# A two-block transformer forward pass: the work region of on-chip memory starts at a multiple of 2,048 bytes

## What is computed

```python
def first_block(x, ...):                     # two layers
    for i in range(2):
        h = x @ w_in[i]                      # q, k, v of three kinds of attention, and gates
        merged = sum(gate_b * (o_b @ w_up_b[i]) for b in (fox, sb, dsa))
        x = layer_norm(ALPHA * x + merged @ w_out[i], ...)
        ffn = jnp.square(jax.nn.relu(x @ w_ff_in[i])) @ w_ff_out[i]
        ple = jax.nn.sigmoid(x @ w_ple_gate[i]) * (p[i] @ w_ple[i])
        x = layer_norm(ALPHA * x + ffn + ple, ...)
    return x

def second_block(x, c, ctx, ...):            # two layers, x and the context xc side by side
    for layer in range(2):
        x  = x  + 0.5 * mx[2] * swiglu(modulate(rms_norm(x, ...), mx[0], mx[1]), w_in, w_out)
        xc = xc + ...                        # the same with the context's modulation
        ox, oc = mla_mixer(...) if layer == 0 else swa_mixer(...)
        x = x + mx[5] * ox                   # and xc
        x = x + 0.5 * mx[8] * swiglu(...)    # and xc, but not in the last layer
    return rms_norm(x, final_norm_g)
```

## The kernel before

| tensor | offset in work, KiB | bytes of one row |
|---|---|---|
| x_hi, x_lo | 0, 8 | 1,024 |
| h_hi, h_lo | 0, 16 | 2,048 |
| un_hi | 32 | 2,048 |
| un_lo | 54.5 | 2,048 |
| f_hi, f_lo | 16, 48 | 1,024 |
| o_hi, o_lo | 59, 65 | 1,024 |
| cq_hi, cq_lo; om_hi, om_lo | 44, 52; 48, 64 | 2,048 |

## Time and profile before

### The profile page before, as it was taken

The page is one execution under the profiler, slowest core; times in us unless marked ns, Lnnn a source line. Parts: engine busy times, 40 slices in busy tenths (PEclk is TensorE's granted clock), DMA queues, the critical chain, the costliest instruction groups (busy, mean ns, idle before and its releaser), DMA issues.

```text
span 3014.3 us, 45553 instructions
## 1 busy us (share of the span) xinstructions
PE 2801.8 (93%) x17432; PEld 2378.3 (79%) x17432; DVE 1566.5 (52%) x2334; ACT 1097.7 (36%) x1415; POOL 0.2 (0%) x4
## 2 busy tenths in 40 slices
PE   7899999999998996999988998999989999889897
PEld 6788799987878995887866576878868788677897
DVE  5676565557765656243255445342353433566555
ACT  3253344334435534223232334222232322335543
POOL 0000000000000000000000000000000000000000
PEclk9999899999998998999999899999999999999998
DMA  8666567585675772242332012242332423311463
GB/s 246 191 206 202 166 218 220 153 253 165 205 249 165 224 215 70 60 118 83 88 92 85 15 43 72 74 114 70 105 96 64 114 77 97 98 56 31 140 187 105
DMA packets 585222, 394.25 MB, mean 131 GB/s; under 512 B 43686, under 2 KB 579140, under 8 KB 584900
## 3 DMA queue, kind: packets, MB, share of 16 engines
q1 hardware_dynamic: 585028, 391.62, 44.0%
HBM read 390.54 MB, written 1.05 MB: 130 GB/s over the span
## 4 chain that ended last, share of the span: by engine, by line
PE 86%; DVE 8%; ACT 3%; issue 2%; DMA 1%; DVEq 0%; ACTq 0%; SPq 0%
PE bank L1856 86%; DVE w_lo L1153 2%; ACT w_hi L849 1%; DMA xs<-in_mod_w 1%; DVE t L1168 1%; DVE xs L1168 1%; DVE t L1161 1%; ACT t L853 0%; DVE h_lo L1168 0%; DMA raw<-in_w_in 0%; DVE qk L1161 0%; DVE acc L1161 0%; DVE t L1165 0%; ACT x_hi L853 0%; ACT h_hi L853 0%
## 5 line engine op out<-in xcount | busy, mean ns | idle before, releaser
L1153 DVE TENSOR_TENSOR w_lo<-raw,w_hi 128x2048 fp32r<-128x2048 f32 (+3 forms) x338 | 689.9, 2041 | 352.9 <-ACT w_hi L849 350.8
L849 ACT CAST w_hi<-raw 128x2048 fp32r<-128x2048 f32 (+3 forms) x338 | 575.0, 1701 | 618.9 <-PE bank L1856 602.4
L1856 PE MATMUL bank<-h_hi,w_hi 128*128 128x512 f32 (+1 forms) x1560 | 574.9, 369 | 52.1 <-DVE h_lo L1168 41.0
L1856 PE MATMUL bank<-h_lo,w_hi 128*128 128x512 f32 (+1 forms) x1560 | 572.9, 367 | 0.0
L1856 PE MATMUL bank<-h_hi,w_lo 128*128 128x512 f32 (+1 forms) x1560 | 572.3, 367 | 0.0
L1856 PE MATMUL bank<-x_hi,w_hi 128*128 128x256 f32 x1344 | 384.1, 286 | 26.6 <-DVE x_lo L1168 13.5
L1856 PEld LDWEIGHTS bank<-h_hi,w_hi 128*128 128x128 f32 x1560 | 297.8, 191 | 113.5 <-issue 48.5
L1856 PE MATMUL bank<-x_lo,w_hi 128*128 128x256 f32 x1344 | 375.8, 280 | 0.0
L1856 PE MATMUL bank<-x_hi,w_lo 128*128 128x256 f32 x1344 | 375.6, 279 | 0.0
L1856 PEld LDWEIGHTS bank<-h_hi,w_lo 128*128 128x128 f32 x1560 | 297.5, 191 | 52.6
L1856 PEld LDWEIGHTS bank<-h_lo,w_hi 128*128 128x128 f32 x1560 | 297.7, 191 | 52.1
(11 more groups left out here) (278 smaller groups left out, 3921.4 us busy)
## 6 DMA issues: line engine op xcount, KB each, us to landing
raw<-in_ffn_w_in SPq DMA_DIRECT2D x176, 512.0 KB
xs<-in_mod_w SPq DMA_DIRECT2D x72, 1024.0 KB, 5.5
raw<-in_ffn_w_out SPq DMA_DIRECT2D x64, 704.0 KB
raw<-in_w_in SPq DMA_DIRECT2D x40, 1024.0 KB
raw<-in_w_ff_in SPq DMA_DIRECT2D x32, 1024.0 KB
raw<-in_w_ff_out SPq DMA_DIRECT2D x32, 1024.0 KB
raw<-in_w_out SPq DMA_DIRECT2D x8, 1024.0 KB
raw<-in_w_ple_gate SPq DMA_DIRECT2D x8, 1024.0 KB
```

The source lines that it names most:

```text
L849: act.copy(w_hi[s][:, w], raw[s][:, w]).then_inc(hi_made, c.did(hi_made))
L1153: dve.tensor_tensor(w_lo[s][:, w], raw[s][:, w], w_hi[s][:, w].bitcast(F32), ALU.subtract).then_inc(lo_made, c.did(lo_made))
L1856: ins = pe.transpose(o, l, r) if transpose else pe.matmul(o, l, r, start=start, stop=stop)
```

## The change

Three of the small tables, `cols_mod` (576 bytes), `cond_st` (1,024) and `small` (256), are no longer allocated among the fixed ones but behind the work region. Together they are 1,856 bytes. Everything that was allocated behind them moves down: `cols_d`, `bf`, `ln_cols`, `mods` by 576, `cond` by 1,600, and `amod` to `top8`, `t1` to `t3`, `rings_8` and `work` by 1,856. `work` becomes 131,072, a multiple of 2,048, and so do `t1` (118,784), `t2` and `t3`. The tensors in the work region keep their offsets in it, so x_hi, h_hi, h_lo, un_hi, f_hi, cq and om now start at multiples of 2,048, o_hi and o_lo (odd KiB) 1,024 above one, and un_lo (54.5 KiB) 512 above one. The chunk slots, `xs` and the constants stay where they are. The three tables now start at 227,328, 227,904 and 228,928. No instruction is added, removed or moved, on any engine: the lists of instructions of both programs, with their waits, are the same row by row.

```diff
@@ -510,18 +510,13 @@
         cols_a = fixed("cols_a", [P, 120])
-        cols_mod = fixed("cols_mod", [P, LAYERS, 72])
         cols_d = fixed("cols_d", [P, 22])
...
-        cond_st = fixed("cond_st", [P, KT, P // COL_GROUPS])
         cond = fixed("cond", [P, 2, KT])
-        small = fixed("small", [P, 64])
-        one = small[:, 2:3]
-        stat = [small[:, 8 + 8 * b:16 + 8 * b] for b in range(3)]
         amod = fixed("amod", [P, KT, 2])
...
         work = top[0]
+        assert work % 2048 == 0
+        top[0] += 94 * 1024
+        cols_mod = fixed("cols_mod", [P, LAYERS, 72])
+        cond_st = fixed("cond_st", [P, KT, P // COL_GROUPS])
+        small = fixed("small", [P, 64])
+        one = small[:, 2:3]
+        stat = [small[:, 8 + 8 * b:16 + 8 * b] for b in range(3)]
+        assert top[0] <= nc.sbuf_usable_end
+        cond_cols = cond_st[:, :, 0:2].rearrange("p k c -> p c k")
...
-        assert work + 94 * 1024 <= nc.sbuf_usable_end, (work, nc.sbuf_usable_end)
```

More of the change, by code:

```diff
@@ L618, in build @@
         ident, ones, rot, fold = (const(cst, n) for n in ("ident", "ones", "rot", "fold"))
-        cond_cols = cond_st[:, :, 0:2].rearrange("p k c -> p c k")
         mod_slot = xs[:, :, S:2 * S]
```

## The result

| | median, us | lowest to highest | runs |
|---|---|---|---|
| before | 3023.21 | 3004.14 to 3029.62 | 6 |
| after | 3036.45 | 3032.36 to 3041.06 | 6 |

The ratio is 1.0056, with a 95% interval of 1.0030 to 1.0082, which is 0.56% or some 17 us; the two medians lie 13 us (0.44%) apart, and against the 75 later runs of the kernel before (median 3018.2 us) the changed one is 18 us slower. The kernel became a little slower: about what the prediction called the least that can be told from no change (0.5%, 15 us), and on the side to which it had given 0.15. The profiled execution took 3036.57 us, its span 3034.8 us, with a mean granted clock of 0.964 (before: 3014.3 us and 0.957).

What follows compares the result with a forecast made beforehand. TensorE's distance between matmul starts was taken to bound the kernel. All terms were 0, added to the profiled 3016.1 us; 3020 us was forecast, between that and the 3021.9 median, with a range of 2930 to 3040.

Steps and rivals of the forecast that it cites:

- The bound: Long stages: TensorE, busy 93% of the span, sets the end by how closely matmuls follow one another.
- The tables, VectorE, ScalarE and the DMAs at 0: Moved tables, vector and scalar work on the region, and transfers: each costed at 0.
- The first two observations against a cost of crossing a multiple of 2,048: Matmul starts: un_lo and un_hi both 0.23 us; 256-column rows, crossing or not, equal within some 3 ns per matmul.
- The moving operand of the matmuls: Streamed rows in the work region: new addresses cost 0; bounds 0 and 90 us gained.
- The prediction's own sign of being wrong: Matmul start distances: wrong if that of 512 or 256 columns moves by more than 3 ns.
- the slower rival: 256-column matmuls: streamed rows at multiples of 128 take 4.4 ns more on 6,816, 30 us, 3050 us; chance 0.15.
- The third argument under it: Matmul surplus of 6.7, 11.1 and 20.0 ns: grows with columns streamed, not a toll at one place of the row.
- The faster rival: 512-column matmuls: aligned rows stop crossing and lose their surplus, 60 to 90 us, some 2945 us; chance 0.42.
- The two rules: Skill on TensorE: N/2.4 + 2.5 ns between matmuls, an estimate of 79 us lower; two read ports independent.

Runs made afterwards that it cites:

- before + 64: The kernel before, tables where they were, with only the work region 64 bytes higher (1920 above a multiple of 2048); 3015.13 us, ratio 0.9988.
- slots and region + 64: The changed kernel with chunk slots and work region both 64 bytes higher; 3036.28 us, ratio 1.0061 to the kernel before.
- slots + 64: The changed kernel with chunk slots 64 bytes higher, work region still at the multiple of 2,048, hgate moved behind it; 3004.23 us, ratio 0.9958.
- region + 64: The changed kernel with only the work region 64 bytes higher, the three tables still behind it; 3009.18 us, ratio 0.9965 to the kernel before.

## Why the prediction was wrong

**What held.** The bound: TensorE alone sets the end, and an address can only matter through the distance between starts. The tables, VectorE, ScalarE and the DMAs at 0: their rows didn't change. The first two observations against a cost of crossing a multiple of 2,048 held as well. Un_lo still crosses and costs what un_hi does, and at "before + 64" every wide row crosses and the wide matmuls have their best pace.

**The step that failed** is the term "The moving operand of the matmuls", costed at 0 "by the nearest rows, those where a crossing can be seen to cost nothing". The rows showed that a crossing costs nothing. They didn't show that an address costs nothing, and the step took the one for the other. The term measured 8,000 times 5.0 ns less 5,310 times 0.6 ns, 40 less 3, some +37 us. The prediction's own sign of being wrong, a distance of 256 columns that moves by more than 3 ns, came about: 5.0 ns, and eighteen starts in 2.13 us, where it had 2.04 for itself and 2.12 for the slower rival. That the 3036 us lie under the 3040 at which its range ended is luck: the range took in only half the way to the slower rival's price, and it held because the time from which its sum starts lies some 15 us above what the distances of the kernel before give.

**The third argument under it** ("the surplus grows with the columns streamed") read 6.7, 11.1 and 20.0 ns as one law. At a distance of 0 both widths have the same surplus, 13.3 ns (120.0 less 106.7, 226.7 less 213.3). From distance 192 to 0 the narrow matmuls lose 6.6 ns and the wide ones gain 6.6. There is no one surplus that an alignment takes away. At half the clock neither width has any: the median distances are 427 and 213 ns, before and after, against 426.7 and 213.3 for the columns alone.

**The slower rival** had the right rows and the right price: 117.6 ns where weights are streamed against 113.3 for activations, 4.4 ns on 6,816 matmuls, 30 us. It measured 5.0 ns on 8,000. Its rule was wrong (the moving operand's residue modulo 128: "slots and region + 64" has the quick residue and 118.7 ns, and "slots + 64" has the region at the same place as the changed kernel and is 32 us quicker). Where weights are streamed past activations, the distance has the other sign, 64 instead of 192, and "slots + 64", which gives the activations that distance, has 117.0 ns: rows 9 were a sample of another distance. The sentence that held it down, that rows 8 show the slow kind at the quick residue as well, was a fact and still is: at distances of 64 and of 192 both kinds occur, while at 0, 128 and 224 no group of 24 starts has a mean under 115 ns. What makes a tile the one or the other at 192 wasn't found. But an exception in a minority of tiles says little against a rival about the majority, and 0.15 was too low for a price read directly off two groups of rows.

**The net of 13 us** (18 against all runs) instead of 37 isn't a correction of the term. It comes of the kernel before, which lies some 15 us above what its distances give (table above); in the profiled pair, 17 us net go to stretches at half the clock. Against "region + 64" the loss is 27 us. The forecast of 3050 for this rival would have stood nearer to the measured time than that of 3020 only by a few us: 14 against 16.

**The faster rival**, crossing as the surplus, gave 2945 us and was wrong in its mechanism: rows of h and un_hi no longer cross and gained 0.6 ns. Yet its thought that 512 columns could be had quicker was right: 6.6 ns of 20.0, by the distance from the loaded weights.

**The two rules.** The best pace of wide matmuls in any run was 226.7 ns and of narrow ones 113.4. The Trainium skill ("TensorE: Matmul & The Clock Gate", section "Back-to-back issue gap") has N/2.4 + 2.5, which is 215.8 and 109.2; no layout tried here reaches either. That section calls the formula the gap of an isolated matmul, which the prediction didn't say, and gives a sustained stream of loads and matmuls about 131 ns at 512 columns; no run here shows such a pace. The Trainium skill ("SBUF — State Buffer", section "Who interferes with whom") lists TensorE's two read ports, for the moving operand and for the weight loads, as independent. Here the pace hangs on the place of the one operand relative to the other: moving the slots alone took 256 columns from 118.8 to 117.0 ns and 512 from 232.7 to 228.9. For the pace the measurement decides. That the two reads meet somewhere is my reading of it; what they meet in, no row shows.

## What to carry to other kernels

Read the pace of a matmul-bound kernel as the mean distance from start to start at full clock, for each width apart, and compare it between layouts. A few per cent can hang on it: in these kernels 226.7 to 233.3 ns and 113.4 to 120.0 ns. Where it does, choose the streamed operand's address relative to the loaded one's, modulo 256, by such a measurement and for each stage by itself. Alignment to a large power of two is no aim in itself. And when rows show that one mechanism costs nothing, that prices that mechanism and not the resource: a rival whose price can be read off directly deserves more than the leftover chance. Before a small difference between two kernels is put down to their code, compare their granted clocks, run by run.

## What the runs showed of the hardware

- With a weight load for each matmul, fp32r operands and the full clock of 2.4 GHz, the distance of 512 columns is 226.7 ns at distance 0, 228.9 at 64, 232.6 at 128 and 233.3 at 192 (modulo 256). That of 256 columns is 119.9, 117.0, 118.7 and 113.8 to 114.5 (113.4 in the quick tiles). The two widths want different layouts. It is the same whether VectorE, ScalarE and the DMAs work or not.
- At half the clock the surplus isn't there at all, at either width (512 columns: 427 ns; 256 columns: 213 ns).
- Crossing a multiple of 2,048 inside a row cost nothing at either width (512 columns: in the changed kernel un_lo crosses and un_hi doesn't, and the mean distances after them are 232.9 and 232.6 ns; 256 columns: the earlier trace rows, to some 3 ns).
- A stretch of 27 us at half the clock in a stage where TensorE doesn't pause cost 11 us of the whole.
- Open: which of the loads a stream meets, since both single-load readings fail; how fine the steps are, since 32 bytes moved 256 columns by 4.9 ns and 512 columns by nothing; why quick and slow tiles stand side by side at distances of 64 and 192; and why the layout of before loses the clock more often. Only fp32r matmuls of these two widths were tried.
